# Four hand-overs between layers of a three-block transformer kernel: another order of normalising, turning and starting the next slab

## What is computed

```python
for i in range(2):
    m = mixer_gdn(x, ...) if i == 0 else mixer_gla(x, ...)        # a_in, a_out / b_qk, b_r, b_v, b_out
    x = layernorm(ALPHA * x + m, ln1_g[i], ln1_b[i])
    x = layernorm(ALPHA * x + matmul(relu(matmul(x, w1[i])) ** 2, w2[i]), ln2_g[i], ln2_b[i])   # up, down
h = rms(x, norm_g) * (1 + scale) + shift; u = h @ w_in            # c_in
x = x + gate * (branches(u, attention(u, context)) @ w_out)       # c_out
```

## Time and profile before

| | before |
|---|---|
| median of 3 runs | 1903.94 us (1903.03 to 1906.78) |
| the profiled execution | 1907.99 us |
| its span | 1905.9 us |
| PE busy in the span | 1838.3 us (96%) |
| DVE, ACT, POOL busy | 987.6, 734.0, 251.8 us |
| granted TensorE clock, mean | 0.988 |

### The profile page before, as it was taken

How to read it: one execution, slowest core, us unless ns; L and a number is a source line. 1 busy time by engine, 2 the same in 40 slices (tenths; PEclk the granted TensorE clock), 3 DMA queues, 4 the chain that set the end, 5 groups by cost and what they waited for, 6 DMA issues and landing times.

```text
span 1905.9 us, 24229 instructions
## 1 busy us (share of the span) xinstructions
PE 1838.3 (96%) x9164; PEld 1484.7 (78%) x9164; DVE 987.6 (52%) x1391; ACT 734.0 (39%) x1207; POOL 251.8 (13%) x246
## 2 busy tenths in 40 slices
PE   8999999999999999999998899999999998998989
PEld 6887798988788888887776687788888887875667
DVE  4775466666654453456321477654443567323653
ACT  4344455554232333333543354232233365344440
POOL 2001344442100000000000153000000000201500
PEclk9999999999999999999999999999999999999999
DMA  5223100000442234322222100443235222420001
GB/s 154 89 88 110 45 2 1 1 1 1 133 133 88 88 95 140 101 98 67 69 86 89 44 1 11 133 151 102 89 110 177 89 89 88 138 77 34 1 1 66
DMA packets 102374, 146.77 MB, mean 77 GB/s; under 512 B 4977, under 2 KB 70721, under 8 KB 102032
## 3 DMA queue, kind: packets, MB, share of 16 engines
q1 hardware_dynamic: 95472, 121.45, 20.2%
q0 software_dynamic: 6816, 24.13, 3.8%
HBM read 143.47 MB, written 2.10 MB: 76 GB/s over the span
## 4 chain that ended last, share of the span: by engine, by line
PE 88%; DVE 5%; ACT 2%; issue 2%; DMA 1%; POOL 1%; DVEq 0%; SPq 0%; ACTq 0%; POOLq 0%
PE bk L278 22%; PE bk L279 21%; PE bk L280 21%; PE bk L1077 2%; PE bk L1095 2%; PE bk L2810 1%; PE bk L2811 1%; PE bk L1086 1%; PE bk L1955 1%; PE bk L2830 1%; PE bk L995 1%; PE bk L1066 1%; POOL work L1498 1%; PE bk L395 1%; PE bk L1013 1%
## 5 line engine op out<-in xcount | busy, mean ns | idle before, releaser
L257 DVE TENSOR_TENSOR wlo<-raw,whi 128x1024 fp32r<-128x1024 f32 x214 | 254.0, 1226 | 390.8 <-ACT whi L251 387.4
L278 PE MATMUL bk<-act_hi,whi 128*128 128x512 f32 x960 | 384.6, 401 | 0.3 <-DVE wlo L730 0.3
L279 PE MATMUL bk<-act_lo,whi 128*128 128x512 f32 x960 | 381.1, 397 | 0.0
L280 PE MATMUL bk<-act_hi,wlo 128*128 128x512 f32 x960 | 381.0, 397 | 0.0
L251 ACT ACTIVATE whi<-raw 128x1024 fp32r<-128x1024 f32 x214 | 216.4, 1054 | 299.6 <-PE bk L280 280.5
L278 PE MATMUL bk<-whi,act_hi 128*128 128x512 f32 x768 | 307.8, 401 | 7.6 <-DVE act_lo L584 4.4
L279 PE MATMUL bk<-wlo,act_hi 128*128 128x512 f32 x768 | 306.6, 399 | 0.0
L280 PE MATMUL bk<-whi,act_lo 128*128 128x512 f32 x768 | 306.2, 399 | 0.0
L278 PEld LDWEIGHTS bk<-act_hi,whi 128*128 128x128 f32 x960 | 180.8, 188 | 48.7 <-issue 4.1
L280 PEld LDWEIGHTS bk<-act_hi,wlo 128*128 128x128 f32 x960 | 180.8, 188 | 44.6
L279 PEld LDWEIGHTS bk<-act_lo,whi 128*128 128x128 f32 x960 | 180.9, 188 | 44.4 <-issue 1.0
(11 more groups left out here) (389 smaller groups left out, 2529.3 us busy)
## 6 DMA issues: line engine op xcount, KB each, us to landing
raw<-in_mlp_w SPq DMA_DIRECT2D x128, 512.0 KB, 4.4
raw<-in_a_w_in SPq DMA_DIRECT2D x32, 512.0 KB, 4.3
work<-in_w_mod POOLq DMA_DIRECT2D x24, 512.0 KB, 3.9
raw<-in_b_w_in SPq DMA_DIRECT2D x24, 512.0 KB, 4.0
raw<-in_w_in SPq DMA_DIRECT2D x14, 512.0 KB, 4.6
raw<-in_a_w_out SPq DMA_DIRECT2D x8, 512.0 KB, 4.2
raw<-in_b_w_out SPq DMA_DIRECT2D x8, 512.0 KB, 4.1
raw<-in_w_out SPq DMA_DIRECT2D x8, 512.0 KB, 3.9
```

The lines of the kernel that those rows point to most:

```text
L257: nc.vector.tensor_tensor(wlo[b][:, hs], raw[hf][:, :], whi[b][:, hs], ALU.subtract).then_inc(w_ready, 1)
L278: nc.tensor.matmul(acc, lhs_hi, rhs_hi, start=first, stop=False, skip_group_check=True)
L279: nc.tensor.matmul(acc, lhs_hi, rhs_lo, start=False, stop=False, skip_group_check=True)
L280: return nc.tensor.matmul(acc, lhs_lo, rhs_hi, start=False, stop=last, skip_group_check=True)
```

## The change

It has five parts. ACT computes 1/std of tile t ahead of the evictions of tile t - 1. DVE takes the second low half of the first slab behind the statistics of tile 0, and the low parts of a turned tile one tile later. Turned tiles have banks (0, 2, 4, 6) and the next one each; tile 0 is turned behind block (1,2), tile 1 behind (0,3), tile 2 behind (1,3). The first slab goes in token pairs of 256. In the last hand-over the turns of the second pair lie between the parts of the first, and DVE's low halves of the slabs are spread out.

```diff
-        def split_lo(dve, k, b):
-            for hf in range(2):
+        def split_lo(dve, k, b, parts=(0, 1)):
+            for hf in parts:
...
-        def split_first_lo(dve, k):
-            for hf in range(2):
+        def split_first_lo(dve, k, parts=(0, 1)):
+            for hf in parts:
...
-        TURN_BANK = (0, 2, 2, 4)
+        TURN_BANK = (0, 2, 4, 6)
...
         def pe_turn_half(pe, e, name, st, hf):
 
             pe.wait_ge(x_ready, 8 * (e - 1) + 2 * st + (hf + 1 if st == 3 else 2))
-            if st == 2:
-                pe.wait_ge(act_ready, 8 * e + 2 + hf + 1)
...
             def between(pe, b, st):
-                if b == 0 and st >= 2:
-                    pe_turn_tile(pe, e, name, st - 2)
+                if (b, st) == (1, 2):
+                    pe_turn_tile(pe, e, name, 0)
+                elif (b, st) == (0, 3):
+                    pe_turn_tile(pe, e, name, 1)
+                elif (b, st) == (1, 3):
+                    pe_turn_tile(pe, e, name, 2)
...
-            if meanwhile is not None and st != 2:
+            if meanwhile is not None:
                 meanwhile()
             dve.wait_ge(st_rstd, 4 * (e - 1) + st + 1)
...
-            if meanwhile is not None and st == 2:
-                meanwhile()
...
         def act_token_end(act, name, e):
             nxt = next_pair(name, PH[name][1] // 2 - 1)
             split_first_hi(act, nxt)
-            for st in range(2):
+            act_norm_tile(act, e, 0)
+            for st in range(1, ST):
                 act_norm_tile(act, e, st)
-                act_turned(act, e, [st])
-            act_norm_tile(act, e, 2)
-            act_turned(act, e, [2])
-            act_norm_tile(act, e, 3)
+                act_turned(act, e, [st - 1])
             act_turned(act, e, [3])
             split_hi(act, nxt, 1)
...
         def dve_token_end(dve, name, e):
             nxt = next_pair(name, PH[name][1] // 2 - 1)
-            split_first_lo(dve, nxt)
-            dve_norm_tile(dve, name, e, 0)
-            for st in range(1, ST):
-                dve_norm_tile(dve, name, e, st, lambda: dve_turned(dve, e, st - 1))
+            split_first_lo(dve, nxt, [0])
+            dve_norm_tile(dve, name, e, 0, lambda: split_first_lo(dve, nxt, [1]))
+            dve_norm_tile(dve, name, e, 1)
+            dve_norm_tile(dve, name, e, 2, lambda: dve_turned(dve, e, 0))
+            dve_norm_tile(dve, name, e, 3, lambda: dve_turned(dve, e, 1))
+            dve_turned(dve, e, 2)
             dve_turned(dve, e, 3)
             split_lo(dve, nxt, 1)
...
             for hf in range(2):
                 pe.wait_ge(w_ready, 2 * PH[name][0] + hf + 1)
                 part(0, range(4 * hf, 4 * hf + 4), 0, 2)
-                if hf == 0:
-                    pe_turn_tile(pe, e, before, 2)
-            pe.wait_ge(act_ready, 8 * e + 6)
-            part(1, range(0, 4), 0, 3)
-            pe_turn_half(pe, e, before, 3, 0)
-            part(1, range(4, 6), 0, 3)
-            pe_turn_half(pe, e, before, 3, 1)
-            part(1, range(6, 8), 0, 3)
-            pe.wait_ge(act_ready, 8 * e + 7)
-            part(0, range(0, 4), 2, 4)
-            part(1, range(0, 4), 3, 4)
-            pe.wait_ge(act_ready, 8 * e + 8)
-            part(0, range(4, 8), 2, 4).then_inc(acc_ready, 1)
-            if middle is not None:
-                middle(pe)
-            part(1, range(4, 8), 3, 4).then_inc(slab_used, 1)
+                pe_turn_half(pe, e, before, 3, hf)
+            part(1, range(0, 8), 0, 2)
+            for hf in range(2):
+                kts = range(4 * hf, 4 * hf + 4)
+                pe.wait_ge(act_ready, 8 * e + 6 + hf + 1)
+                mm = part(0, kts, 2, 4)
+                if hf == 1:
+                    mm.then_inc(acc_ready, 1)
+                    if middle is not None:
+                        middle(pe)
+                mm = part(1, kts, 2, 4)
+            mm.then_inc(slab_used, 1)
...
         def dve_c_norm(dve):
-            split_first_lo(dve, nxt)
-            for st in range(ST):
+            split_first_lo(dve, nxt, [0])
+            dve_norm_tile(dve, "down1", 4, 0, lambda: split_first_lo(dve, nxt, [1]))
+            for st in range(1, ST):
                 dve_norm_tile(dve, "down1", 4, st)
             for i in (8, 9):
                 dve_c_low(dve, i)
-            split_lo(dve, nxt, 1)
-            for i in range(10, 24):
+            split_lo(dve, nxt, 1, [0])
+            for i in range(10, 16):
+                dve_c_low(dve, i)
+            split_lo(dve, nxt, 1, [1])
+            for i in range(16, 24):
                 dve_c_low(dve, i)
...
             for m in range(4):
                 pe_c_turn(pe, 0, m)
-            for m in range(2):
-                pe_c_turn(pe, 1, m)
...
-            for m in range(2):
-                part(0, m)
-            for m in range(2, 4):
-                pe_c_turn(pe, 1, m)
-            for m in range(2, 4):
+            for m in range(4):
                 part(0, m)
+                for m2 in ((0, 1), (2,), (3,), ())[m]:
+                    pe_c_turn(pe, 1, m2)
             for m in range(4):
                 part(1, m)
```

## The result

The changed kernel takes 1894.26 us (median of 8 runs, 1886.5 to 1898.2) against 1903.72 beside it (8 runs): ratio 0.9936, 95% interval 0.992 to 0.9952, 12.2 us faster by the ratio. The two medians themselves lie 9.5 us apart, a ratio of 0.995, which the interval also holds. Its profiled execution took 1898.16 us (span 1896.1), 9.8 less than the one of before.

A forecast was written before the change was run, and what follows sets the result against it. PE, holding 88% of the chain, bounds the kernel. Hand-over gains sum to 15.5 us without clock falls, 10.7 with falls in hand-overs 1 to 3; 13.1 off the median 1903.94 gives 1890.8 us, range 1886.0 to 1898.5 (a little over 80%).

The forecast's parts named there:

- the stops ahead of turn 0: Hand-overs 1 and 3: PE's stops of 1.97 and 1.75 us ahead of tile 0's turn disappear.
- the stop ahead of the slab: Hand-over 1: PE waits 1.95 us for tile 1's low parts, where 2.3 to 2.4 was, and resumes at 521.15.
- The stop of 0.5 ahead of turn 2: Hand-over 1: PE waits 0.5 us for normalised X of tile 2, ready at 518.3.
- The re-cut: First slab's column j = 1 in 256-token pieces: 1.2 us less in each of three hand-overs; nothing by the skill page's rule.
- Hand-overs: Gains without a clock fall, or with one: hand-over 1 6.7 or 5.1 us; 2 and 3 each 3.7 or 2.1.
- I take half: Hand-overs 1 to 3: clock falls behind three of six stops before, so 13.1 us between 15.5 without and 10.7 with falls.
- Hand-over 4: Last hand-over: part(0,0) starts at low part 9, 1610.7 instead of 1612.27; gain 1.4 us, low clock's 2.3 us stays.
- is what removes the 3.10 us wait: Hand-over 1, DVE: ACT's root ahead of evictions removes the wait at 520.08; tile 1's low parts end at 521.1, before 523.95.
- (1): Rival, 18%: the stop ahead of the first slab grows, PE resumes about where it did; gain 7 us, 1897.
- rival 2: 7%: gain given back later, an event that does not move with PE holds it; 1900 to 1904.
- (3): Rival, 5%: the clock stays low through the first slabs, 11.5 us slower, 1915.
- (4): Rival, 8%: all clock falls vanish, hand-over 4's too; 17.8 us faster, 1886.

The follow-up runs named there:

- after again: Second timing and profiled execution of the unaltered changed kernel, against the kernel before: 1889.58 us, ratio 0.9925.
- after: First timing and profiled execution of the changed kernel, against the kernel before: 1894.26 us, ratio 0.9936; the profiled execution took 1898.16 us.
- modmix: Changed kernel with the modulation's two-column matmuls spread four at a time between the last half slab's products: 1890.21 us, ratio 0.9934 to before.
- u_act: Changed kernel with ACT's 1/std root behind the evictions again: 1896.17 us, ratio 0.9957 to before.
- u_last: Changed kernel with PE's order in hand-over 4 as before: 1891.9 us, ratio 0.9932 to before.
- u_cut: Changed kernel with column j = 1 of the first slab in pieces of 384 and 128 again: 1896.7 us, ratio 0.9961 to before.
- u_first: Changed kernel with both low halves ahead of tile 0's add again: 1895.58 us, ratio 0.9957 to before.
- u_turn2: Changed kernel with tile 2's turn back inside the first slab, tile 3's half turns later in it: 1895.85 us, ratio 0.9946 to before.
- number 6: The run u_last: changed kernel with PE's order in hand-over 4 as before; 1891.9 us, ratio 0.9932 to before.
- number 9: Kernel before with only ACT's new order, the next tile's statistics ahead of the evictions: 1904.29 us, ratio 0.9996 to before.
- number 1: The run u_act: changed kernel with ACT's 1/std root behind the evictions again; 1896.17 us, ratio 0.9957 to before.
- number 12: Changed kernel with ACT's order and the place of DVE's low parts both undone: 1902.15 us, ratio 0.9982 to before.
- number 3: Changed kernel with tile 1's low parts ahead of tile 3's add, tile 3's half turns later in the slab: 1882.52 us, ratio 0.9894 to before.

## Why the prediction was right

- **The bound and the stops.** PE bounds; the stops ahead of turn 0 in hand-overs 1 and 3 are gone, and the stop ahead of the slab stayed at 2.0 where 1.95 was forecast. Resume at 520.85; forecast 521.15 from a block that began 0.14 later, so 0.16 off. The stop of 0.5 ahead of turn 2 did not come: tile 0's add started at 502.25, not 502.7, and X of tile 2 was ready at 517.71, when PE arrived. That the resume came out so close is partly luck: DVE was 0.6 us ahead of the forecast (518.3), and then tile 3's add waited until 517.94 for its sum on PE, a wait that the sum did not have.
- **The first slab.** 12.25 to 12.26 us without a fall in after again (forecast 12.4), 13.9 with one (14). The re-cut: 1.07 to 1.46, forecast 1.2. That it could be worth nothing, which the prediction had set against the row, is not borne out.
- **Hand-overs.** 5.3, 3.7 and 2.1 measured where 5.1 (fall), 3.7 (no fall) and 2.1 (fall) stood; in after again 7.0, 2.2 and 3.8 where 6.7, 2.1 and 3.7 stood.
- **Falls: "I take half".** In eight profiled executions of changed kernels with a stop of 1.7 to 3 us ahead of the first slab (after, after again, modmix, u_act, u_last, u_cut, u_first, u_turn2), three hand-overs each, a fall lies in H1 to H3 in 12 of 24. In the three kernels without the stop it is 0 of 9. The section "A second HAM failure mode: psum-queue depth-cycling" of the page "TensorE: Matmul & The Clock Gate" of the Trainium skill says that short idles between groups of matmuls, if frequent enough, make the clock swing. In these eleven executions the falls of hand-overs 1 to 3 came only where the stop stood, which agrees; that every hand-over falls, as I had read it, is not what the runs show.
- **Hand-over 4** was mis-sized: 1.4 forecast, 2.1 measured (41.36 against 43.47). PE resumes 1603.15 - 1578.39 = 24.76 us behind the stretch's start, before 1612.27 - 1586.04 = 26.23: 1.5 earlier, close to the 1.4. The term that was off is the low clock, which was to stay at 2.3 us and cost 1.7 behind the stop (0.64 over 4.77 us). That is chance too: in u_first, with the same code there, it cost 3.1 (0.58 over 7.46 us) and H4 is 42.67. Of the 1.5, about 0.8 is PE's order (number 6); the other 0.7 fits the moved low half (0.65), which was not tried alone there.
- **The step that does not hold** is the worth of the sentence that the root ahead of the evictions "is what removes the 3.10 us wait". The wait does go (number 9: 3.10, 1.91 and 1.92 us become 0.57), but the time does not follow (ratio 0.9996): the low parts of tile 0, in their old place, then wait 0.99 us, and except in hand-over 1, where the clock had fallen, PE resumes only 0.2 us earlier behind turn 0. Taken out of the whole change the same order costs 2.5 us a hand-over (number 1), and together with the place of the low parts 3.6 (number 12). What shortens DVE's chain is the two orders together, with turn 0 one block later. The sum came out right because I had computed DVE's and PE's chains in the changed order as a whole, where both edits stand.
- **The rivals.** The stop did not grow (1). Stretches between the hand-overs were longer by 3.7 us in the profiled execution, which looks like rival 2, but 3.1 of it lies where the clock falls behind the two-column block. The clock did not stay low (3): in the hand-overs of both profiles its low stretches lasted under 6 us. Not all falls vanished (4); with number 3 none is left in hand-overs 1 to 3. That is the best of the versions run: 1882.5 us, 20 under before by the ratio, against 12 to 14 for the change.

What stays open: why a stop of 2.0 us brings the clock down in one execution and not in the next, and what brings it down in "to H3" and "rest", which no edit touches.

## What to carry to other kernels

Reordering three engines at a hand-over is one edit, not three: price the chain in the final order, since undoing single parts costs 2.5, 1.2, 1.0 and 0.8 us a hand-over on the average, and 3.6 for a pair, where the whole gives 3.8 without falls (32.08 against 28.31). When a stop is left, ask which work stands ahead of the releasing instruction on its engine: moving tile 1's low parts ahead of one add gave 6 to 8 us where the whole change gave 12 to 14. Where the clock falls by chance behind short stops, compare stretches at the same state of the clock, and read a second profile of the same kernel before calling a difference of 1.6 us an effect.

## What was unexpected of the hardware

Behind the same stop of 2.0 us the clock was at 0.60 for 4 us in one execution and at 1.00 in another of the same kernel. Around a block of 32 two-column matmuls (3.3 to 4.4 us) the clock cost 0, 1.6 or 3.2 us (335.7, 337.3, 338.9): nothing in 5 of the 24 passes of the twelve profiled executions that have the block, one such loss in 13, two in 6. With four of them at a time between full products it stayed at 1.00 in 4 of 4. A 128-column piece costs 0.112 us where a 256-column one costs 0.118, confirmed by 3.6 us in three hand-overs.
